# A recurrent mixer's engine queues reordered: reciprocals in halves, the gate in one piece, the decay scan one level later

## The reference, cut to what matters

```python
def wkv7_scan(r, w, k, v, a, b):
    """S_t = S_{t-1} diag(w_t) + (S_{t-1} a_t) b_t^T + v_t k_t^T ; y_t = S_t r_t."""
...
def rwkv7_mixer(r, k, v, dw, da, dg, w0, w2, a0, a2, g2, k_k, k_a, r_k, gn_w, gn_b):
    w_log = -jax.nn.softplus(-(w0 + jnp.tanh(dw) @ w2).astype(f32)) - 0.5
    decay = jnp.exp(-jnp.exp(w_log))
    a = jax.nn.sigmoid((a0 + da @ a2).astype(f32))
    g = (jax.nn.sigmoid(dg) @ g2).astype(f32)
    kk = (k * k_k).astype(f32).reshape(B, S, H, N)
    kk = kk / jnp.maximum(jnp.sqrt(jnp.sum(kk * kk, axis=-1, keepdims=True)), 1e-12)
    k = k.astype(f32) * (1.0 + (a - 1.0) * k_a.astype(f32))
    y = wkv7_scan(rh, wh, kh, vh, -kk, kk * ah)
    mu = jnp.mean(y, axis=-1, keepdims=True)
    var = jnp.mean(jnp.square(y - mu), axis=-1, keepdims=True)
    y = ((y - mu) * lax.rsqrt(var + GN_EPS)).reshape(B, S, C) * gn_w + gn_b
    bonus = jnp.sum(rh * kh * r_k.astype(f32), axis=-1, keepdims=True) * vh
    y = y + bonus.reshape(B, S, C)
    return (y * g).astype(r.dtype)
```

## Time and profile before

| | |
|---|---|
| time of the runs, median (lowest to highest) | 3263.35 us (3263.17 to 3270.22), 3 runs |
| profiled execution | 3260.77 us, span 3258.7 us |
| instructions | 57483 |
| busy: PE, DVE, ACT, POOL | 3138.0 (96%), 1681.2 (52%), 1033.4 (32%), 1968.5 (60%) us |
| chain that ended last | PE 84%, DVE 9%, ACT 5% |
| the mixer's stage | about 262 to 760 us |

### The profile page before, as it was taken

The page is one execution under the profiler, slowest core; times in us unless marked ns, Lnnn a source line. Parts: engine busy times, 40 slices in busy tenths (PEclk is TensorE's granted clock), DMA queues, the critical chain, the costliest instruction groups (busy, mean ns, idle before and its releaser), DMA issues.

```text
span 3258.7 us, 57483 instructions
## 1 busy us (share of the span) xinstructions
PE 3138.0 (96%) x20978; PEld 2472.2 (76%) x20978; DVE 1681.2 (52%) x2722; ACT 1033.4 (32%) x1860; POOL 1968.5 (60%) x2607
## 2 busy tenths in 40 slices
PE   7999999999999999999999999999999999999999
PEld 4767666678888886677778888877667778888887
DVE  4457777754553345525545644445551634555345
ACT  2153333321211113634443411123551536231112
POOL 4624333348688855254646888876336374898886
PEclk9999999999999999999999999999999999999999
DMA  5442111113233322022222333332113121333333
GB/s 213 143 161 60 42 41 47 41 54 117 69 97 97 99 74 71 27 66 65 65 66 72 91 97 97 97 92 83 40 35 90 45 84 46 94 94 97 97 97 97
DMA packets 70805, 265.42 MB, mean 81 GB/s; under 512 B 7744, under 2 KB 7872, under 8 KB 67520
## 3 DMA queue, kind: packets, MB, share of 16 engines
q1 hardware_dynamic: 68288, 257.59, 25.9%
q10 hardware_dynamic: 2304, 4.83, 0.4%
HBM read 260.29 MB, written 2.10 MB: 81 GB/s over the span
## 4 chain that ended last, share of the span: by engine, by line
PE 84%; DVE 9%; ACT 5%; issue 2%; DMA 1%; SPq 0%; DVEq 0%; ACTq 0%
PE psum_a L587 11%; PE psum_a L590 11%; PE psum_a L591 11%; PE psum_d L587 6%; PE psum_d L590 6%; PE psum_d L591 6%; PE psum_d L653 5%; PE psum_a L745 3%; PE psum_d L1119 2%; PE psum_d L848 2%; PE psum_a L775 2%; PE psum_a L779 2%; PE psum_a L778 2%; PE psum_a L616 1%; PE psum_a L619 1%
## 5 line engine op out<-in xcount | busy, mean ns | idle before, releaser
L3356 POOL TENSOR_TENSOR w_lo<-raw,w_hi 128x256 fp32r<-128x256 f32 x1736 | 1422.4, 850 | 36.2
L3350 POOL TENSOR_TENSOR mark<-mark 128x1 f32<-128x1 f32 x432 | 103.5, 240 | 1208.6 <-PE psum_a L587 610.8
L587 PE MATMUL psum_a<-h_hi,w_hi 128*128 128x512 f32 x1632 | 654.9, 401 | 6.2 <-ACT arena L1700 6.2
L591 PE MATMUL psum_a<-h_hi,w_lo 128*128 128x512 f32 x1632 | 636.9, 390 | 0.0
L590 PE MATMUL psum_a<-h_lo,w_hi 128*128 128x512 f32 x1632 | 636.9, 390 | 0.0
L3351 POOL TENSOR_SCALAR w_hi<-raw 128x1024 fp32r<-128x1024 f32 x434 | 460.9, 1062 | 33.1 <-DMA raw<-in_weights 33.1
L587 PEld LDWEIGHTS psum_a<-h_hi,w_hi 128*128 128x128 f32 x1632 | 306.6, 188 | 84.3 <-issue 11.0
L591 PEld LDWEIGHTS psum_a<-h_hi,w_lo 128*128 128x128 f32 x1632 | 306.8, 188 | 65.5
L590 PEld LDWEIGHTS psum_a<-h_lo,w_hi 128*128 128x128 f32 x1632 | 307.0, 188 | 61.5 <-issue 2.4
L587 PE MATMUL psum_d<-split,w_hi 128*128 128x512 f32 x848 | 329.9, 389 | 0.0
L590 PE MATMUL psum_d<-split,w_hi 128*128 128x512 f32 x848 | 329.9, 389 | 0.0
(11 more groups left out here) (374 smaller groups left out, 5272.9 us busy)
## 6 DMA issues: line engine op xcount, KB each, us to landing
raw<-in_weights SPq DMA_DIRECT2D x434, 512.0 KB, 3.6
plain<-in_ada SPq DMA_DIRECT2D x20, 1024.0 KB, 7.0
arena<-in_ada SPq DMA_DIRECT2D x4, 1024.0 KB, 16.8
x<-in_x SPq DMA_DIRECT2D x1, 2048.0 KB, 12.0
x<-in_x ACTq DMA_DIRECT2D x1, 2048.0 KB, 10.4
out<-x SPq DMA_DIRECT2D x8, 256.0 KB, 3.4
arena<-in_pe ACTq DMA_DIRECT2D x2, 512.0 KB, 3.8
const<-in_const ACTq DMA_DIRECT2D x1, 906.0 KB, 8.6
```

The lines of the kernel that those rows point to most:

```text
L587: m = pe.eng.matmul(dst, wh, hi(t), start=t == 0, stop=False)
L591: m = pe.eng.matmul(dst, wl, hi(t), start=False, stop=t == k - 1)
L3350: eng.tensor_tensor(b.mark[:, 1:2], b.mark[:, 0:1], b.mark[:, 0:1], ALU.add)
L3356: m = eng.tensor_tensor(lo[:, part], b.raw[:, s, part], hi[:, part].bitcast(F32), ALU.subtract)
```

## The change

No arithmetic changes, apart from one reciprocal of 512 columns that becomes two of 256. The order changes:

- PE: the gate's eight parts stand together, ahead of the transitions, in the next bank; of the rkv product one part fewer stands before level 1 and one more in it; the keys R_KH are turned behind the map products.
- ACT: the gate's sigmoid stands before the copies of the chunk outputs; the decays move from level 2 to level 3, behind the copy of R's projection.
- DVE: the deviation's reciprocal is done in halves, one before and one behind the transitions, and the scaling follows; "mixed" moves from level 3 to before level 1; the scan moves from the end of level 1 to the end of level 2; the other input steps move: 3 to before level 3's additions and 5 behind them, the shift of R in two parts, the first half of the keys' reciprocal to level 5, the second behind the maps.

```diff
 def pe_rwkv(pe, j, chain):
...
     if chain:
         chain.inputs()
-    gate = PePieces(pe, "gate", 2 if chain else 0)
-    gate.part(4)
+    pe_features(pe, "a", "gate", H)
     if chain:
         chain.maps()
-    gate.part(4)
...
-    piece.part(5)
+    piece.part(4)
...
-        piece.part(1 if k == 1 else 2)
+        piece.part(2)
...
-    for src in (b.R_V, b.R_BH, b.R_KH):
-        turned = pe_turned(pe, [src[:, q * P:(q + 1) * P] for q in range(NQ)])
+    for src in (b.R_V, b.R_BH):
+        pe_turned(pe, [src[:, q * P:(q + 1) * P] for q in range(NQ)])
     pe_units(pe, "d", (B, R))
     maps = pe_units(pe, "d", (K, lambda v, row, out: AR[ROWS[row], 2 * v + out]), width=P)
+    turned = pe_turned(pe, [b.R_KH[:, q * P:(q + 1) * P] for q in range(NQ)])
...
 def act_rwkv(a, j):
...
         act_rwkv_inputs(a)
+    act_first_gate(a, b.x[:, j])
+    if j:
         act_rwkv_outputs(a)
-    act_first_gate(a, b.x[:, j])
...
         if k == 2 and more:
-            act_rwkv_decays(a)
             act_rwkv_squares(a, j + 1)
         if k == 3 and more:
+            act_rwkv_decays(a)
             act_rwkv_length(a)
...
 def dve_rwkv_input(v, j, step):
...
     if step == 4:
-        dve_shift(v, n + 1, b.R_R, j)
+        dve_shift_change(v, n + 1)
+    if step == 6:
+        dve_shift_mixed(v, n + 1, b.R_R, j)
...
+    if step == 11:
         v.eng.wait_ge(v.sem[v.last], v.own())
         v.eng.reciprocal(b.R_SW[:, 0:T // 2], b.R_SW[:, 0:T // 2]).then_inc(v.sem["dve_step"], v.up("dve_step"))
...
 def dve_rwkv(v, j):
...
     dve_rwkv_prepare(v, j)
+    if j >= 2:
+        dve_rwkv_inverse(v, 0)
     if j:
         dve_rwkv_transitions(v, j - 1)
+    if j >= 2:
+        dve_rwkv_inverse(v, 1)
+        dve_rwkv_normed(v, j - 2)
...
     if j >= 2:
-        dve_rwkv_normed(v, j - 2)
+        dve_rwkv_mixed(v, j - 2)
...
         if k > 1 and more:
-            dve_rwkv_input(v, j + 1, (2, 5, 4, 10)[k - 2])
+            dve_rwkv_input(v, j + 1, (2, 3, 4, 11)[k - 2])
...
-        if k in (1, 2, 4) and more:
-            dve_rwkv_input(v, j + 1, (1, 3, 0, 8)[k - 1])
-        if k == 3 and j >= 2:
-            dve_rwkv_mixed(v, j - 2)
+        if k in (2, 3, 4) and more:
+            dve_rwkv_input(v, j + 1, (1, 5, 6)[k - 2])
+        if k == 4 and more:
+            dve_rwkv_input(v, j + 1, 8)
...
     dve_rwkv_maps(v)
     if more:
+        dve_rwkv_input(v, j + 1, 10)
         dve_rwkv_input(v, j + 1, 9)
         dve_rwkv_input(v, j + 1, 7)
...
+def dve_rwkv_inverse(v, half):
+
+    std = v.b.R_STD[:, half * T // 2:(half + 1) * T // 2]
+    if half == 0:
+        v.eng.wait_ge(v.sem["gn_std"], v.due("gn_std"))
+    v.eng.wait_ge(v.sem[v.last], v.own())
+    v.eng.reciprocal(std, std).then_inc(v.sem["dve_step"], v.up("dve_step"))
...
 def dve_rwkv_normed(v, j):
     b = v.b
-    v.eng.wait_ge(v.sem["gn_std"], v.due("gn_std"))
-    v.eng.wait_ge(v.sem[v.last], v.own())
-    v.eng.reciprocal(b.R_STD, b.R_STD).then_inc(v.sem["dve_step"], v.up("dve_step"))
```

More of the change, by code:

```diff
@@ L2791, in dve_shift, with dve_shift_change @@
 def dve_shift(v, n, dst, mu):
+    dve_shift_change(v, n)
+    dve_shift_mixed(v, n, dst, mu)
+def dve_shift_change(v, n):
     b = v.b
@@ L2797, in dve_shift, with dve_shift_mixed @@
     v.eng.tensor_tensor(b.R_T, u[:, 0:T], u[:, 1:T + 1], ALU.subtract).then_inc(v.sem["dve_step"], v.up("dve_step"))
+def dve_shift_mixed(v, n, dst, mu):
+    b = v.b
+    u = b.R_U[:, n % 2]
     v.eng.wait_ge(v.sem[v.last], v.own())
@@ L3201, in dve_program @@
             .then_inc(v.sem["act_lo"], v.up("act_lo"))
-    for step in (1, 2, 3, 5, 4, 8, 10, 9, 7):
+    for step in (1, 2, 3, 5, 4, 6, 8, 11, 10, 9, 7):
         dve_rwkv_input(v, 0, step)
```

## The result

| | before | after |
|---|---|---|
| median (lowest to highest), 15 runs each | 3263.13 us (3261.37 to 3270.22) | 3272.0 us (3269.35 to 3275.98) |
| ratio to before, 95% interval | | 1.0029 [1.0022, 1.0036] |
| profiled execution (span) | 3260.77 us (3258.7) | 3269.35 us (3267.5) |

The kernel became 8.9 us slower, 0.29%. I had forecast 3263.6 with a range of 3253 to 3270, so the time lies outside. The reciprocal's halves are L2653.

The account below looks back on a forecast made before the run. TensorE (PE) was taken as the bound, busy 466.13 of the recurrent stage's 498.00 us. Group terms +0.6 - 1.5 + 1.5 - 0.3 = +0.3 gave 3261.1 profiled, 3263.6 as median; range 3253 to 3270.

Parts of the forecast that it names:

- +1.4 - 2.45 + 1.66 - 0.38 - 0.1 = +0.1: Sum for each of groups 2 to 6: pair product, levels, level 4, level 5, maps; five groups, +0.6 us.
- forecast of +0.3: All groups of the stage together: +0.6 - 1.5 + 1.5 - 0.3 = +0.3 us.
- The second pair product: Head of a group: PE waits for L2577's bank, starting at 15.3 us, before at 13.9: 1.4 us lost.
- The levels: Levels 1 to 3: PE's waits for DVE's masks and additions vanish, 2.45 us a group gained.
- Level 4, ACT: Decays delay ACT's turned inverse, so PE newly waits 1.66 us before level 4's second product; bounds 0.4 and 1.7.
- Rival 1: ACT's wait in level 4 does not appear: 3251.0 us, faster by 0.4%; chance 0.13.
- rival 3: A second ACT table load in a row costs more than its 1.28 us: 3272.6 us; chance 0.02.
- Level 5 and the maps: Level 5's mask wait goes, -0.38 us; the keys' turning behind the maps gives -0.1, bounds 0 and -0.3.
- Group 1: No reciprocal, so the head's gain stays: -0.7 - 2.1 + 1.66 - 0.4 = -1.5 us.
- Group 0: Level 4's second product +2.65 us, less 0.9 of level waits and 0.3 in level 5: +1.5.
- Group 7: No next keys, so no decays: +1.4 - 1.7 (its wait in level 1) = -0.3 us.
- Rival 2: DVE behind the maps is the new bound, costing more than priced, at L2577: 3273 us; chance 0.07.

Follow-up runs that it names:

- runs 11 and 12: Second profiles of the unchanged kernels after and before: after 3264.65 us in its single run, beside 3262.98 for before there; before 3262.48 us.
- run 4: The kernel after with two small DVE copies between the scaling and the gate's product, lengthening PE's wait: 3279.45 us, ratio 1.0049.
- runs 4 and 5: The kernel after with two small DVE copies lengthening PE's wait, 3279.45 us; and with the first pair product computed three times to fill it, 3266.05 us.
- Run 1: The kernel after with ACT's decays back in level 2, behind the squares: 3262.35 us, ratio 1.0003.
- run 9: The kernel before with only the turning of the keys moved behind the maps: 3264.42 us, ratio 1.0005.
- runs 1 to 6: The kernel after with, in turn, decays back; reciprocal half later; both; longer DVE wait; wait filled; shorter half: ratios 1.0003, 1.0014, 0.9971, 1.0049, 1.0011, 1.0013.
- run 3: The kernel after with decays back in level 2, and the reciprocal's second half and scaling behind the inverse's first value: 3251.86 us, ratio 0.9971.
- run 10: The kernel after with decays in level 2, reciprocal's second half behind the inverse's first value, scaling behind level 1, mixed behind level 3, keys' turning undone: 3241.5 us, ratio 0.9939.

## Why the prediction was wrong, point by point

**The step that failed** is the rule by which the sum was made: every wait of PE was priced by its length alone. "+1.4 - 2.45 + 1.66 - 0.38 - 0.1 = +0.1" for a group trades short waits for two long ones, and by length it is even. It was: added up from the trace, PE's waits in groups 2 to 6 are 23.08 us before and 23.10 after, where I had +0.6. For the whole stage it is +0.7 against a forecast of +0.3. The stage grew by 6.8 us all the same: 0.7 of idle time, 1.7 by the turning and 4.4 by slow matmuls. What the sum lacked is a term for what follows a wait. After has seven waits of 2.3 to 2.8 where before has three of 1.7 to 1.8. At the rate of the table (about half are followed, by 1.3 to 2.0 us) those are worth some 6 us against 2.5, an estimate. With the 1.7 of the turning and the 0.7 of idle time that is 6, of the 8.9 measured. The other 3 are not explained; in the first pair of profiles 2.3 us stand ahead of the stage. That a slow stretch costs time beyond the wait is shown within one kernel (0.8 to 1.6 us a group, table of runs 11 and 12) and by the groups of run 4. The times of runs 4 and 5, 4 us beyond the length one way and 5.9 the other, point the same way, but the first isn't clear of the noise and the second rests on after's ratio. The range had no such term either, and its upper end of 3270 rested on the scatter of before.

**The second pair product** (+1.4): right in place and cause. PE waited there for L2585, at 15.06 (15.4 in groups 2 and 3) and not 15.3. The scaling took 0.75 and not 0.91. The first half did cost nothing: DVE still idled 2.04 ahead of the transitions.

**The levels** (-2.45): the masks' waits vanished as worked out. The additions' did not wholly: in groups 1, 3 and 5 level 3's first product waits 0.95 for L2618. It isn't the scan, which starts behind that addition and takes 1.23 there; it is the shift of K ahead of it, whose two passes take 1.18 and 1.11 in these groups and 0.69 and 0.75 in groups 2, 4 and 6. Before had waits there of 0.6 to 0.8. In the five groups it evened out against smaller terms.

**Level 4, ACT** (+1.66): 1.60 measured, 2.76 in group 0 (2.65). Run 1 shows it: with the decays back, this wait falls under 1.0 and 8.5 us return. Rival 1 did not come about; both loads began behind the copy of R. Nor did rival 3: the root began 0.02 behind its load of 1.28. For the Trainium skill, "ScalarE: Activation LUTs", What ACT_TABLE_LOAD costs, a switch has a drain of some 1380 ns besides; behind two loads in a row the trace shows none.

**Level 5 and the maps** (-0.38, -0.1): the first is right. The second had the wrong sign: -0.1 forecast, 0.23 to 0.32 more measured in each of groups 1 to 6 of run 9, some 2 us of the stage. The keys' turning saves PE a wait of 0.3 for L1700, pays 0.21 for the variance and 0.2 in busy time, which I had not counted. That the 0.2 is for the switches between forms is my reading; no run separates it.

**Group 1** (-1.5): -0.1 measured, by the same count of waits (3.92 to 3.82). The gate's 0.69, the mask's 1.32 and level 5's 0.37 went, but the wait for the additions grew from 0.80 to 0.95 where I took it as gone, 0.47 with no releaser appeared, and level 4's 1.59 came. With its busy time group 1 is 0.26 longer than before, so 1.8 of the 6.5 us by which the stage missed are here, by waits and turning alone. Group 0 gave +1.3 (+1.5 forecast), and 1.5 more by slow matmuls. Group 7 gave -0.6 (-0.3).

**Rival 2**, DVE behind the maps with more than I priced, came nearest in time (3273) and is not what happened: L2585 was not late. The change costs there through what PE does afterwards. That parts of the change were worth having was in none of my cases: the gate alone gives 6.2 us, and with the decays back in level 2 and the reciprocal's second half behind the inverse's first value the whole is 0.29% faster than before.

**What stays open**: why one wait of 2.3 us is followed by slow matmuls and the next of the same length is not. Between two profiles of the same kernel the places changed while the waits stayed. And the single second run of after was 1.7 above the median of before beside it, not 8.9, with a stage 3.9 longer than the second one of before. One run can't say what of that is luck with the stretches and the early start, and what is the chip: that after's ratio is the same on every chip was not tested, and runs 1 to 6 are compared with it.

## What to carry to other kernels

Price a wait of the bound engine by its length only while it is short. Where an edit merges several short waits of TensorE into one of two or more microseconds, look in the trace for slow matmuls behind waits of that length, in every profile that there is, and add their loss to the sum. Compare groups of one kernel, with and without them, before trusting medians of two kernels. And test the parts of a bundled change alone: here one was worth 6 us and two misplaced ones hid it. Putting these two right turned 0.29% slower into 0.29% faster (run 3), and spreading "mixed" again and undoing the turning made that 0.61% (run 10).

## What the runs showed of the hardware that was not expected

- Behind a wait of PE of 1.7 to 3.05 us, some of the time, matmuls of 512 columns start 0.43 us apart and not 0.23, for some 2 to 6 us, at a granted clock that reads 0.50 where the stretch asked for (run 1, 430 to 435) lies wholly inside: TensorE's lower level, 1.2 of 2.4 GHz. Within one kernel it made a group 0.8 to 1.6 us longer. Of 57 such waits 29 were followed so; behind the shorter ones none was, such as the six of 1.6 us in each profile of after. The Trainium skill, "TensorE: Matmul & The Clock Gate", HAM oscillation — how this bites in real kernels, tells of a kernel in which each wait between groups of matmuls lets the next group start at the lower clock; the trace agrees that it happens, and shows that here it is a matter of the single execution.
- Matmuls that repeat a finished product, which shortened waits of 2.3 to 2.65 to 1.2 to 1.4 in five groups (1.71 in a sixth), left no slow stretch behind those five; group 3, slow in after, became 1.5 us shorter, and groups that were not slow in after stayed as long. PE's extra work there cost no time.
- The same 288 turns took 1.7 us more busy time when 32 of them, the keys', stand behind products of 64 rows and not beside other turns.
- An ACT table load of 1.28 us was followed by its function 0.01 to 0.02 us later, also where two loads start 2.66 us apart (519.63 and 522.29).
